# The last layer's two lanes put 33 steps apart instead of 48, with their marks at multiples of three

## The chip, the cores and the metric

The kernel runs on one core of one Trainium2 chip. The time is the device time of one execution in microseconds (us); what counts is the median of several executions.

## What is computed

Four transformer-like layers over 256 tokens of width 2048, batch 1, in float32. Only the fourth (`odd_layer`) is touched by the change. Cut to what matters:

```python
def odd_layer(x, ...):
    proj = rmsnorm(x, norm_g) @ w_in
    xc, zc, qd, kd, vd, zd, a_pre, b_pre = split_cols(proj, OD_SIZES)
    xconv = causal_dwconv(xc, conv_c_w) + conv_c_b
    yc = rg_lru(xconv, gate_w, gate_b, lam) * silu(zc)
    q, k, v = split(silu(causal_dwconv(concat([qd, kd, vd]), conv_d_w)))
    q, k = l2norm(q), l2norm(k)                       # 8 heads of 128
    od = gated_delta_chunkwise(q, k, v, beta, g)
    yd = rmsnorm(od, onorm_g) * silu(zd)
    return concat([yc, yd]) @ w_out
```

`rg_lru` is an elementwise linear recurrence over the tokens. `gated_delta_chunkwise` needs, for each head, the inverse of a unit lower triangular matrix and then a short chain of products with it.

## The kernel before

**Weights.** Nearly all the work of PE is the product of the activations with weights that come from HBM once. SP fetches them unit by unit (half a MB each, two DMAs) into `raw`. ACT rounds each half of a unit to fp32r (L1359, into `whi`), DVE subtracts it from the original (L1993, into `wlo`), and PE does three products for each block of 128 rows and each of the two token blocks: L676, L677, L678. ACT works three halves ahead of PE and may start on a half once PE is done with the half four before it. SP waits, before it fetches unit u, until DVE has split the last half of unit u-4 (`lo_done`).

**The order is written out by hand.** Every engine has its own program, and in it the main work calls `next(side)` at fixed places. The side is a set of generators. In the last layer it is `lanes(...)`, and one call of it is here called a **step**. With `fine=True` every engine makes four steps for each half of a unit, so PE does three of the big products (L676 to L678) in each step, a `project` (one slab of 512 columns) is 32 steps, and the twelve slabs are steps 0 to 383. Where an engine's side has nothing to do at a step it goes on at once; where it has a semaphore to wait for, the engine waits, with all its later work queued behind it, the main work too. PE does nothing out of this order, nor do ACT and DVE.

**The lanes.** `lanes` has three lists of (step at which it may begin, generator). Lane 0 does the gates, then the recurrences of pairs 0 and 2 (`lru`), then the delta rule of pairs 0 and 2 (`delta`); lane 1 does pairs 1 and 3 in the same way; a pair is two heads. The third list multiplies y by the gate z (`gated`). Inside `lru` and `delta`, `to(n)` waits until the generator's own step n; every engine has the same generator with marks of its own, so they stay in the same order. In `lru`, lane 0 stretches its marks by 4/3 and lane 1 by 2.

**A pair of `delta`, by its own steps before:** PE turns q and k (0) and v (4); DVE does nine convolution taps as pairs of L2620 and the three silus (L2672) from 4 to 29; ACT does the first taps (L1875), the tanhs (L1890), and at 23 the squares of q (L1887), which wait for the silu of k. PE sums squares and does k times k at 30 (L1250, L1255), and turns v at 36. At 34 DVE reads the decays (L2696, L2697, L2700), which it needs from DRAM; ACT takes their exponentials at 37 (four L1896, eight of L1904 and L1902). PE does the q-k products at 42 and 49 (L1262 to L1264); the one at 49 waits for DVE's four L2723. From 56 the inverse is built in six rounds. A round l is a product "z" (L1236, with four transposes L1285 behind it from the second round on), a mask by DVE (L2738), a product "t" (L1236), and copies by ACT (L1912 of t, L1916 of the transposes). z stands at 53+6l and t at 56+6l, so each product comes three steps after the one before it, and between them one other engine must have done its part. Then come the solves at 96, 99, 102 (L1295, L1300, L1305) and the output product at 107 (L1312); DVE ends the pair at 114 (L2769), and the lane's next pair waits for that.

**The decays.** `decays` is a small DRAM tensor; each pair needs one row of it on all partitions, in a tile `B` that lies where the pair's convolution inputs were. SP issues that copy (L636) between weight units, at the units numbered 24, 30, 39 and 45 of the layer for pairs 0 to 3:

```python
                if u >= 4:
                    sp.wait_ge(lo_done, 2 * (u - 4) + 2)
                ...
                if u in decays_at:
                    pair = decays_at.index(u)
                    sp.wait_ge(rows_out[1], 16)
                    sp.wait_ge(*dl_d[pair % 2].at(pair // 2, "vc"))
                    sp.dma_start(flat(L3.lane[pair % 2].B), row(decays[2 * pair], 2 * S)).then_inc(dec_in[pair], 16)
```

Half h of the layer's slabs is split by DVE just before its step 4(h-3)+2, and unit n's wait is for half 2n-7. So the copies can go out from steps 8n-38 on: 154, 202, 274 and 322. `vc` is the last tap of v, at the pair's own step 22.

**Gates.** `gated(n)` is one DVE operation over 128x1024 (L2844) at steps 302, 324, 356 and 388, and two over 128x512 (L2852) two steps later (much later for the last). The tanh before it is ACT's L1971.

Of the kernel before, what the change touches and what calls it, by code (L numbers as in the profile page):

```python
# [102 lines left out]
def lanes(gates, delta, lru, gated):  # L103

    lane = [[(0, gates()), (40, lru(0)), (86, lru(2)), (132, delta(0)), (250, delta(2))],
            [(48, lru(1)), (114, lru(3)), (180, delta(1)), (298, delta(3))],
            [(302, gated(0)), (324, gated(1)), (356, gated(2)), (388, gated(3))]]
    tick = 0  # L110
    while any(lane):
        for side in lane:
            if side and tick >= side[0][0] and next(side[0][1], "over") == "over":
                del side[0]
        tick += 1
        yield
# [44 lines left out]
def build_program(nc, a, out, layers=(0, 1, 2, 3)):  # L161
    assert tuple(layers) == (0, 1, 2, 3)
    ctx = ExitStack()
    with ctx:
# [499 lines left out]
        def tensor(pe):  # L664
# [563 lines left out]
            def delta(pair):  # L1228
# [12 lines left out]
                for n in range(3):  # L1241
                    if n == 2:
                        yield from to(4)
                        pe.wait_ge(*v3_a.at(r, "v"))
                        pe.wait_ge(*da.at(r, "cp0"))
                    four(b + n % 2, lambda hh, tb: v.staged[:, n, tb, hh * P:(hh + 1) * P]).then_inc(*dp.up(f"turn{n}"))
# [21 lines left out]
                behind_keys(0, b).then_inc(*dp.up("qk0"))  # L1268
                yield from to(49)
                pe.wait_ge(*dd.at(r, "ad"))  # L1270
                behind_keys(1, b + 1).then_inc(*dp.up("qk1"))
                yield from to(56)
                pe.wait_ge(*dd.at(r, "m"))
# [5 lines left out]
                for l in range(1, 7):  # L1279
                    yield from to(53 + 6 * l)  # L1280
                    pe.wait_ge(*da.at(r, f"mt{l - 1}"))
                    four_by_four(b, v.AD, v.Mt).then_inc(*dp.up(f"z{l}"))
                    if l > 1:
                        for n in range(4):
                            m = pe.transpose(ps[:, b + 1, n * P:(n + 1) * P], v.Mt[:, n, :], ident[:, :])  # L1285
                        m.then_inc(*dp.up(f"d{l - 1}"))
                    yield from to(56 + 6 * l)
                    pe.wait_ge(*dd.at(r, f"z{l}"))
                    if l > 1:
                        pe.wait_ge(*da.at(r, f"m{l - 1}"))  # L1290
                    four_by_four(b, v.M, v.Z).then_inc(*dp.up(f"t{l}"))
# [14 lines left out]
                m.then_inc(*dp.up("u1"))  # L1306
                yield from to(107)
                pe.wait_ge(*dd.at(r, "u1"))
# [36 lines left out]
        def scalar(act):  # L1345
# [511 lines left out]
            def delta(pair):  # L1857
# [47 lines left out]
                m.then_inc(*da.up("ext"))  # L1905
                yield from to(56)
                act.wait_ge(*dp.at(r, "mt"))
                act.copy(flat(v.Mt), ps[:, b, :]).then_inc(*da.up("mt0"))
                for l in range(1, 7):
                    yield from to(56 + 6 * l)  # L1910
                    act.wait_ge(*dp.at(r, f"t{l}"))
                    act.copy(flat(v.Mt), ps[:, b, :]).then_inc(*da.up(f"mt{l}"))  # L1912
                    if l < 6:
                        yield from to(58 + 6 * l)
                        act.wait_ge(*dp.at(r, f"d{l}"))
                        act.copy(flat(v.M), ps[:, b + 1, :]).then_inc(*da.up(f"m{l}"))  # L1916
# [66 lines left out]
        def vector(dve):  # L1983
# [670 lines left out]
            def delta(pair):  # L2654
# [80 lines left out]
                for l in range(1, 7):  # L2735
                    yield from to(53 + 6 * l)
                    dve.wait_ge(*dp.at(r, f"z{l}"))
# [14 lines left out]
                dve.tensor_copy(v.u[:, :, 1], two(b)).then_inc(*dd.up("u1"))  # L2752
                yield from to(107)
                dve.wait_ge(*dp.at(r, "o"))
# [297 lines left out]
```

## Time and profile before

| | |
|---|---|
| median of 3 runs | 2406.24 us (2406.13 to 2406.74) |
| the profiled execution | 2405.99 us |
| its span in the trace | 2404.3 us |
| TensorE's granted clock | 1.0 of full speed |
| PE busy | 2394.9 us (100%) |
| DVE busy | 1478.7 us (62%) |
| ACT busy | 1185.3 us (49%) |
| POOL busy | 150.6 us (6%) |
| mean DMA rate | 174 GB/s |

The span leaves out 1.7 us of start and end that lie around it. Busy times are sums over an engine's instructions; since one instruction's record can reach into the next one's, the distance from start to start is what an instruction takes of its engine when they stand back to back.

### The profile page before, as it was taken

What the parts mean: (1) busy time and instruction counts of PE and PEld (TensorE: products, weight loads), DVE (VectorE), ACT (ScalarE), POOL (GpSimd) and SP (SyncE); (2) the same over time, 40 slices, a digit from 0 to 9 for tenths busy, and PEclk for the clock granted to TensorE, in tenths of its full rate; (3) what the DMA queues carried; (4) which work ended last, traced back from release to release, by engine and by line L of the source; (5) the groups of instructions that cost most, each with busy time, mean ns of one, the idle gap of its engine ahead of it and who ended that gap; (6) DMA issues with size and microseconds to landing.
All of it is one profiled execution on the core that took longest, in us unless ns stands there. A gap on an engine that the chain in (4) does not pass through costs nothing.

```text
span 2404.3 us, 31344 instructions
## 1 busy us (share of the span) xinstructions
PE 2394.9 (100%) x12582; PEld 2043.7 (85%) x12582; DVE 1478.7 (62%) x1982; ACT 1185.3 (49%) x1641; POOL 150.6 (6%) x130
## 2 busy tenths in 40 slices
PE   9999999999999999999999999999999999999999
PEld 8888888888888888878899878888888888888887
DVE  6757575757575757575556576555445566757754
ACT  5454444444444444445455456455444368745543
POOL 0201010101010101000000000000000010000000
PEclk9999999999999999999999999999999999999999
DMA  8555555555555555556654556555555565534444
GB/s 265 177 174 189 197 184 169 186 169 186 168 186 169 185 168 175 194 165 198 189 144 136 193 158 202 179 178 194 176 177 173 173 198 164 160 124 128 127 140 140
DMA packets 369278, 418.26 MB, mean 174 GB/s; under 512 B 28198, under 2 KB 298764, under 8 KB 368620
## 3 DMA queue, kind: packets, MB, share of 16 engines
q1 hardware_dynamic: 367788, 409.36, 52.5%
q0 software_dynamic: 1344, 6.89, 0.8%
q8 instruction: 99, 1.62, 0.3%
q14 instruction: 47, 0.39, 0.1%
HBM read 414.09 MB, written 2.11 MB: 173 GB/s over the span
## 4 chain that ended last, share of the span: by engine, by line
PE 97%; DVE 1%; ACT 1%; issue 0%; POOL 0%; DVEq 0%; POOLq 0%; ACTq 0%
PE ps L676 19%; PE ps L678 19%; PE ps L677 19%; PE ps L707 15%; PE ps L706 7%; PE ps L1236 2%; PE ps L748 2%; PE ps L960 1%; PE ps L949 1%; PE ps L1012 1%; PE ps L1013 1%; PE ps L1011 1%; PE ps L954 1%; PE ps L779 1%; PE ps L781 0%; PE ps L780 0%
## 5 line engine op out<-in xcount | busy, mean ns | idle before, releaser
L1993 DVE TENSOR_TENSOR wlo<-raw,whi 128x1024 fp32r<-128x1024 f32 (+1 forms) x760 | 943.6, 1251 | 611.2 <-ACT whi L1359 608.1
L1359 ACT CAST whi<-raw 128x1024 fp32r<-128x1024 f32 (+1 forms) x766 | 793.3, 1041 | 703.2 <-PE ps L678 522.9
L676 PE MATMUL ps<-whi,xx 128*128 128x512 f32 x2064 | 821.8, 398 | 0.0
L678 PE MATMUL ps<-whi,xx 128*128 128x512 f32 x2064 | 805.2, 390 | 0.0
L677 PE MATMUL ps<-wlo,xx 128*128 128x512 f32 x2064 | 803.8, 389 | 0.0
L707 PE MATMUL ps<-xx,whi 128*128 128x512 f32 x1536 | 538.6, 396 | 0.2 <-DVE wlo L1993 0.2
L678 PEld LDWEIGHTS ps<-whi,xx 128*128 128x128 f32 x2064 | 387.4, 188 | 82.7
L677 PEld LDWEIGHTS ps<-wlo,xx 128*128 128x128 f32 x2064 | 388.2, 188 | 75.6
L676 PEld LDWEIGHTS ps<-whi,xx 128*128 128x128 f32 x2064 | 387.9, 188 | 74.8
L706 PE MATMUL ps<-xx,wlo 128*128 128x256 f32 x1440 | 405.4, 282 | 0.0
L707 PEld LDWEIGHTS ps<-xx,whi 128*128 128x128 f32 x1536 | 286.2, 188 | 63.3 <-issue 0.4
L706 PEld LDWEIGHTS ps<-xx,wlo 128*128 128x128 f32 x1440 | 271.6, 189 | 2.0
L2900 POOL TENSOR_TENSOR work<-work 128x512 f32<-128x512 f32 x48 | 96.7, 2014 | 830.1 <-DVE work L2335 627.2
L1501 ACT ACTIVATE work<-work,small 128x128 f32<-128x128 f32 (+1 forms) x80 | 44.4, 555 | 143.3 <-DVE small L2233 143.3
L2331 DVE TENSOR_TENSOR work<-work 64x512 f32<-64x512 f32 x96 | 88.4, 921 | 2.2
L1605 ACT COPY work<-ps 128x512 f32<-128x512 f32 x48 | 28.0, 584 | 59.9 <-PE ps L707 59.9
L2370 DVE TENSOR_TENSOR work<-work,ps 128x512 f32<-128x512 f32 x48 | 33.0, 687 | 36.7 <-ACT work L1605 36.7
L1236 PEld LDWEIGHTS ps<-work 128*128 128x128 f32 x384 | 49.7, 191 | 5.0 <-ACT work L1912 1.3
L1236 PE MATMUL ps<-work 128*128 128x128 f32 x384 | 50.9, 275 | 0.3
L2230 DVE CUSTOM_DVE_ANT_0 work<-ps,work 128x128 f32<-128x128 f32 (+1 forms) x80 | 36.0, 488 | 21.0 <-PE ps L949 15.6
L1011 PE MATMUL ps<-xx,whi 128*128 128x256 f32 x160 | 48.1, 301 | 0.0
L1013 PE MATMUL ps<-xx,whi 128*128 128x256 f32 x160 | 45.2, 283 | 0.0
(428 smaller groups left out, 1897.8 us busy)
## 6 DMA issues: line engine op xcount, KB each, us to landing
raw<-in_dsa_w_in SPq DMA_DIRECT2D x320, 512.0 KB, 4.4
raw<-in_ev_w_in SPq DMA_DIRECT2D x144, 512.0 KB, 4.4
raw<-in_od_w_in SPq DMA_DIRECT2D x96, 512.0 KB, 4.6
raw<-in_mla_w_in SPq DMA_DIRECT2D x48, 512.0 KB, 4.5
raw<-in_dsa_w_out SPq DMA_DIRECT2D x32, 512.0 KB, 4.7
raw<-in_mla_w_out SPq DMA_DIRECT2D x32, 512.0 KB, 4.8
raw<-in_ev_w_out SPq DMA_DIRECT2D x32, 512.0 KB, 4.5
raw<-in_od_w_out SPq DMA_DIRECT2D x32, 512.0 KB, 4.8
```

The source lines that it names most:

```text
L676: pe.matmul(o, xh[:, k, tokens[tb]], hi, start=start and s + l == 0, stop=False)
L677: pe.matmul(o, xh[:, k, tokens[tb]], lo, start=False, stop=False)
L678: m = pe.matmul(o, xl[:, k, tokens[tb]], hi, start=False, stop=stop and s + l == 2)
L706: pe.matmul(ps[:, bank + c, 0:S], lo[:, t, cols], xh[:, k, :], start=False, stop=False)
L707: m = pe.matmul(ps[:, bank + c, :], hi[:, t, cols], xx[:, :, k, :], start=k == 0, stop=k == KT - 1)
L1011: pe.matmul(o, hi, xh[:, k, :], start=first and g != 1, stop=False)
L1013: m = pe.matmul(o, hi, xl[:, k, :], start=False, stop=last and g != 0)
L1236: m = pe.matmul(ps[:, bank, n * P:(n + 1) * P], left[:, n, :], right[:, n, :], start=True, stop=True)
L1359: act.copy(half_of_weights(h)[0][:, :, 0:n] if n > FEW else few_high(h, n), whole_half(raw[:, u % 4, 2 * (h % 2):2 * (h % 2) + 2], n)).the ...
L1993: dve.tensor_tensor(lo[:, :, 0:n] if n > FEW else few_low(h, n), whole_half(raw[:, h // 2 % 4, 2 * (h % 2):2 * (h % 2) + 2], n), hi.bitcas ...
L2331: m = dve.tensor_tensor(L0.t2[a_], L0.h[b_, n], bc(L0.sina[b_], 1, 2), ALU.mult)
L2900: pool.tensor_tensor(L0.t1, L0.h[:, n], bc(L0.cosa, 1, 2), ALU.mult).then_inc(*p0_g.up(f"cos{n}"))
```

## The change

Two things are edited, both of them only numbers that say at which step something stands. In `lanes`, `lru(2)`, `delta(0)` and `delta(2)` of lane 0 start at 89, 138 and 255 instead of 86, 132 and 250, and `lru(1)`, `lru(3)`, `delta(1)` and `delta(3)` of lane 1 at 40, 105, 171 and 288 instead of 48, 114, 180 and 298. So the delta pairs are 33 steps apart, which was 48. Inside `delta` the marks of PE's products go to multiples of three, with the marks of DVE and ACT that belong to them: v is turned at 3, the second q-k product stands at 48, the first transposes at 57, z at 54+6l, t at 57+6l, the output product at 108. No instruction is added, taken away or changed in size, and `decays_at` and the steps of `gated` stay.

```diff
-    lane = [[(0, gates()), (40, lru(0)), (86, lru(2)), (132, delta(0)), (250, delta(2))],
-            [(48, lru(1)), (114, lru(3)), (180, delta(1)), (298, delta(3))],
+    lane = [[(0, gates()), (40, lru(0)), (89, lru(2)), (138, delta(0)), (255, delta(2))],
+            [(40, lru(1)), (105, lru(3)), (171, delta(1)), (288, delta(3))],
             [(302, gated(0)), (324, gated(1)), (356, gated(2)), (388, gated(3))]]
...
                     if n == 2:
-                        yield from to(4)
+                        yield from to(3)
                         pe.wait_ge(*v3_a.at(r, "v"))
...
-                yield from to(49)
+                yield from to(48)
                 pe.wait_ge(*dd.at(r, "ad"))
                 behind_keys(1, b + 1).then_inc(*dp.up("qk1"))
-                yield from to(56)
+                yield from to(57)
                 pe.wait_ge(*dd.at(r, "m"))
...
                 for l in range(1, 7):
-                    yield from to(53 + 6 * l)
+                    yield from to(54 + 6 * l)
                     pe.wait_ge(*da.at(r, f"mt{l - 1}"))
...
-                    yield from to(56 + 6 * l)
+                    yield from to(57 + 6 * l)
                     pe.wait_ge(*dd.at(r, f"z{l}"))
...
-                yield from to(107)
+                yield from to(108)
                 pe.wait_ge(*dd.at(r, "u1"))
```

ACT's marks of the same loop go from 56+6l and 58+6l to 57+6l and 59+6l, DVE's from 53+6l to 54+6l and from 107 to 108.

**Where the instructions go.** On SP nothing moves. On PE the number of places at which the layer's big products are interrupted by small ones falls from 108 to 85, since products of both lanes now stand at the same place 23 times. Three places show what moves on DVE and ACT.

DVE around `gated(0)` (step 302), where pair 2 is past its four L2723. Before (L2730 and L2734 are pair 2's, L2620 pair 3's taps):

```order
L2730 TENSOR_TENSOR work<-ps,work 128x512 [waits dl_a0,dl_p0]
L1993 TENSOR_TENSOR wlo<-raw,whi 128x1024 [waits hi_done]
L2734 TENSOR_TENSOR work<-work 128x512 [waits dl_g0]
L2730 TENSOR_TENSOR work<-ps,work 128x512 [waits dl_a0,dl_p0]
L1993 TENSOR_TENSOR wlo<-raw,whi 128x1024 [waits hi_done]
L2620 SCALAR_TENSOR_TENSOR work<-work,vec 128x256 [waits dl_a1]
L2620 SCALAR_TENSOR_TENSOR work<-work,vec 128x256
L2844 SCALAR_TENSOR_TENSOR work<-work,ps 128x1024 [waits z3_a]
L2620 SCALAR_TENSOR_TENSOR work<-work,vec 128x256 [waits z3_d,dl_d1,rg_a1,rg_a0]
L2620 SCALAR_TENSOR_TENSOR work<-work,vec 128x256
L2852 SCALAR_TENSOR_TENSOR y<-work,hrstd,y 128x512 x2
```

Now:

```order
L2620 SCALAR_TENSOR_TENSOR work<-work,vec 128x256 [waits dl_a1]
L2620 SCALAR_TENSOR_TENSOR work<-work,vec 128x256
L2730 TENSOR_TENSOR work<-ps,work 128x512 [waits dl_a0,dl_p0]
L2620 SCALAR_TENSOR_TENSOR work<-work,vec 128x256 [waits dl_d1]
L2620 SCALAR_TENSOR_TENSOR work<-work,vec 128x256
L1993 TENSOR_TENSOR wlo<-raw,whi 128x1024 [waits hi_done]
L2620 SCALAR_TENSOR_TENSOR work<-work,vec 128x256 [waits dl_d1]
L2620 SCALAR_TENSOR_TENSOR work<-work,vec 128x256
L2844 SCALAR_TENSOR_TENSOR work<-work,ps 128x1024 [waits z3_a]
L2672 SCALAR_TENSOR_TENSOR work<-work 128x512 [waits dl_a1,dl_d1]
L2734 TENSOR_TENSOR work<-work 128x512 [waits z3_d,dl_g0,rg_a1,rg_a0]
L2852 SCALAR_TENSOR_TENSOR y<-work,hrstd,y 128x512 x2
```

Before, pair 3 had just begun here and two of its three taps of q are shown; now its taps of k and v and its silu of q stand among the same work of pair 2, and an L1993 fewer lies between.

ACT around the first copy of pair 2's inverse (L1908). Before:

```order
L1875 ACTIVATE work<-work,vec 128x256 [waits dl_a1]
L1875 ACTIVATE work<-work,vec 128x256
L1908 COPY work<-ps 128x512 [waits dl_p0]
L1890 ACTIVATE work<-work 128x512 [waits dl_d1]
L1359 CAST whi<-raw 128x1024 [waits half_done,raw_in3]
L1912 COPY work<-ps 128x512 [waits dl_p0]
L1359 CAST whi<-raw 128x1024 [waits half_done,raw_in3]
L1916 COPY work<-ps 128x512 [waits dl_p0]
L1890 ACTIVATE work<-work 128x512 [waits dl_d1]
```

Now:

```order
L1890 ACTIVATE work<-work 128x512 [waits dl_d1]
L1359 CAST whi<-raw 128x1024 [waits half_done,raw_in2]
L1359 CAST whi<-raw 128x1024 [waits half_done,raw_in3]
L1887 ACTIVATE work<-work 128x512 [waits dl_d1]
L1908 COPY work<-ps 128x512 [waits dl_p0]
L1890 ACTIVATE work<-work 128x512 [waits dl_d1]
L1359 CAST whi<-raw 128x1024 [waits half_done,raw_in3]
L1359 CAST whi<-raw 128x1024 [waits half_done,raw_in0]
L1912 COPY work<-ps 128x512 [waits dl_p0]
```

Before, the first taps of pair 3 (L1875) stood ahead of that copy; now the squares of pair 3's q (L1887) do, which wait for DVE's silu of k (`dl_d1`).

DVE around the split for which SP waits before it fetches pair 3's decays. Before, the six rows from that L1993 on; pair 3's L2696 comes 16 rows further down:

```order
L1993 TENSOR_TENSOR wlo<-raw,whi 128x1024 [waits hi_done]
L2844 SCALAR_TENSOR_TENSOR work<-work,ps 128x1024 [waits z3_a]
L1993 TENSOR_TENSOR wlo<-raw,whi 128x1024 [waits z3_d,hi_done,rg_a1,rg_a0]
L2852 SCALAR_TENSOR_TENSOR y<-work,hrstd,y 128x512 x2
L2738 TENSOR_TENSOR work<-ps,work 128x512 [waits dl_p0]
L2672 SCALAR_TENSOR_TENSOR work<-work 128x512 [waits dl_a1,dl_d1]
```

Now:

```order
L2738 TENSOR_TENSOR work<-ps,work 128x512 [waits dl_p0]
L1993 TENSOR_TENSOR wlo<-raw,whi 128x1024 [waits hi_done]
L2696 TENSOR_TENSOR small<-work 128x2 [waits dl_d1,dec_in3]
L2697 SCALAR_TENSOR_TENSOR work<-work 128x512
L2700 TENSOR_TENSOR work<-work 128x2x128 x2
L2844 SCALAR_TENSOR_TENSOR work<-work,ps 128x1024 [waits z3_a]
L2708 SCALAR_TENSOR_TENSOR small<-small,work 128x4 [waits dl_g1]
L2710 SCALAR_TENSOR_TENSOR small<-small 128x4 [waits dl_d1]
L2712 TENSOR_SCALAR small<-small 128x2 [waits dl_d1]
L2713 TENSOR_SCALAR small<-small 128x4
L1993 TENSOR_TENSOR wlo<-raw,whi 128x1024 [waits z3_d,hi_done,rg_a1,rg_a0]
L2716 TENSOR_TENSOR work<-ps,small 128x512 [waits dl_p1]
```

The second row is the same L1993. L2696, which waits for the decays (`dec_in3`), now stands right behind it, with L2844, the next L1993, L2716 and L2852 behind that and pair 2's next L2738 after them.

## Rows read from the trace of the kernel before

**Rows 1.** The page: its first line, and the chain that ended last.

```profile
span 2404.3 us, 31344 instructions
...
PE 97%; DVE 1%; ACT 1%; issue 0%; POOL 0%; DVEq 0%; POOLq 0%; ACTq 0%
```

**Rows 2.** Groups by line, PE, last layer (busy, mean ns | idle before, releaser).

```profile
L1236 PE MATMUL ps<-work 128*128 128x128 f32 x384 | 50.9, 275 | 0.3
...
L748 PE MATMUL ps<-ident,work 128*128 128x128 f32 x80 | 11.3, 272 | 0.5 <-DVE y L2769 0.5
```

**Rows 3.** PE in order of time: a side product and the big products behind it.

```profile
2097.28 1.05 PE L1236 MATMUL ps<-work 128*128 128x128 f32 x8
2098.08 0.48 PE L676 MATMUL ps<-whi,xx 128*128 128x512 f32 x1
2098.40 0.39 PE L677 MATMUL ps<-wlo,xx 128*128 128x512 f32 x1
2098.63 0.39 PE L678 MATMUL ps<-whi,xx 128*128 128x512 f32 x1
```

**Rows 4.** PE in order of time: output product joined across lanes, and one alone.

```profile
2149.48 1.50 PE L1312 MATMUL ps<-work 128*128 128x128 f32 x12
2150.82 1.06 PE L1236 MATMUL ps<-work 128*128 128x128 f32 x8
...
2202.03 1.50 PE L1312 MATMUL ps<-work 128*128 128x128 f32 x12
2203.28 0.48 PE L676 MATMUL ps<-whi,xx 128*128 128x512 f32 x1
```

**Rows 5.** DVE in order of time: three kinds of work back to back.

```profile
2181.36 0.69 DVE L2672 SCALAR_TENSOR_TENSOR work<-work 128x512 f32<-128x512 f32 x1
2181.97 1.22 DVE L1993 TENSOR_TENSOR wlo<-raw,whi 128x1024 fp32r<-128x1024 f32 x1
2183.10 1.80 DVE L2620 SCALAR_TENSOR_TENSOR work<-work,vec 128x256 f32<-128x256 f32 x4
2184.89 0.69 DVE L2738 TENSOR_TENSOR work<-ps,work 128x512 f32<-128x512 f32 x1
```

**Rows 6.** ACT in order of time: the exponentials of pair 3 (eight follow 2252.48).

```profile
2252.48 1.28 ACT L1896 ACTIVATE work<-work 128x128 f32<-128x128 f32 x4
2253.66 0.39 ACT L1904 ACTIVATE work<-work,small 128x128 f32<-128x128 f32 x1
...
2256.00 0.57 ACT L1912 COPY work<-ps 128x512 f32<-128x512 f32 x1
2256.47 1.05 ACT L1359 CAST whi<-raw 128x1024 fp32r<-128x1024 f32 x1
```

**Rows 7.** SP, PE and DVE around the decays of pair 3.

```profile
2239.36 0.34 SPq L636 DMA_DIRECT2D work<-decays  x1
...
2235.01 1.05 PE L1236 MATMUL ps<-work 128*128 128x128 f32 x8
...
2236.10 0.69 DVE L2738 TENSOR_TENSOR work<-ps,work 128x512 f32<-128x512 f32 x1 [1.23 <-PE ps L1236]
2238.11 1.23 DVE L1993 TENSOR_TENSOR wlo<-raw,whi 128x1024 fp32r<-128x1024 f32 x1 [1.31 <-ACT whi L1359]
2239.25 1.22 DVE L2844 SCALAR_TENSOR_TENSOR work<-work,ps 128x1024 f32<-128x1024 f32 x1
...
2247.68 0.16 DVE L2696 TENSOR_TENSOR small<-work 128x2 f32<-128x2 f32 x1
...
2248.37 0.75 DVE L2700 TENSOR_TENSOR work<-work 128x256 f32<-128x256 f32 x2
```

**Rows 8.** DMA issues of the last layer (KB each, median us to landing).

```profile
work<-decays SPq DMA_DIRECT2D x4, 256.0 KB, 4.3
```

**Rows 9.** Groups by line, DVE, last layer.

```profile
L2723 DVE SCALAR_TENSOR_TENSOR work<-ps,small,work 128x128 f32<-128x128 f32 x16 | 4.5, 343 | 0.0
...
L2852 DVE SCALAR_TENSOR_TENSOR y<-work,hrstd,y 128x512 f32<-128x512 f32 x8 | 5.6, 747 | 0.0
```

More of the change, by code:

```diff
@@ L1905, in delta @@
                 m.then_inc(*da.up("ext"))
-                yield from to(56)
+                yield from to(57)
                 act.wait_ge(*dp.at(r, "mt"))
@@ L1909, in delta @@
                 for l in range(1, 7):
-                    yield from to(56 + 6 * l)
+                    yield from to(57 + 6 * l)
                     act.wait_ge(*dp.at(r, f"t{l}"))
@@ L1913, in delta @@
                     if l < 6:
-                        yield from to(58 + 6 * l)
+                        yield from to(59 + 6 * l)
                         act.wait_ge(*dp.at(r, f"d{l}"))
@@ L2735, in delta @@
                 for l in range(1, 7):
-                    yield from to(53 + 6 * l)
+                    yield from to(54 + 6 * l)
                     dve.wait_ge(*dp.at(r, f"z{l}"))
@@ L2752, in delta @@
                 dve.tensor_copy(v.u[:, :, 1], two(b)).then_inc(*dd.up("u1"))
-                yield from to(107)
+                yield from to(108)
                 dve.wait_ge(*dp.at(r, "o"))
```

## The prediction

> **What bounds the kernel now.** I read the page first: PE is the chain that ended last in 97% of a span of 2404.3 us [rows 1], so the time is PE's own work plus what PE waits. Then the groups by line, for PE's waits in the last layer: 0.5 at L748, where pair 3's first turn waits for pair 1's L2769, 0.3 at L1236 [rows 2], and some 0.2 more spread over single rows. About 1.0 us is all that better marks could take from the waits. Then PE in order of time, for what an interruption costs: the 8 products of a z or t take 0.80, and the L676 behind them starts its successor 0.32 later where L677 has 0.23, so a return to the big products costs 0.09; a step of three big products is 3 x 0.228 = 0.685 [rows 3]. Last DVE, ACT and SP around pair 3, since the change moves lane 1's start onto busy stretches of lane 0.
>
> **Joining the lanes' products** (108 places become 85). If each of the 23 places saved that 0.09, it would be 2.1 us. The trace has such a joint already: the output product with the other lane's L1236 behind it takes 1.34, the same product with L676 behind it 1.25 [rows 4]. The 0.09 is thus paid at the border between the lanes too, and joining saves nothing but the restart of the big product, some hundredths at a few places. I take 0.1 in all; bounds 0 and 2.1. The Trainium skill (TensorE: Matmul & The Clock Gate, "Part 2: What happens when you issue a matmul") says that products in a stream cost only their columns and an isolated one shows its drain; by it the joins would be worth the 2.1, and the sum below would be 14.6 in place of 16.6.
>
> **The waits of before.** Pair 2's four L2723 (1.1) stood on DVE in the steps just ahead of pair 1's L2769; with lane 1 fifteen steps earlier against lane 0 they now come after it, a silu (0.61) is there, and the 0.5 at L748 goes. The other 0.5 I count as gone too: -1.0.
>
> **New stalls.** What replaces them comes from one fact. Lane 1's first own steps are its dearest for DVE and ACT (nine tap pairs, three silus, twelve first taps, three tanhs). 48 steps behind, they lay where lane 0 was in its inverse, which leaves DVE free. 33 behind, own steps 0 to 24 of lane 1 are 33 to 57 of lane 0: its decays, exponentials, L2723s and copies. What one thing costs, start to start: a silu or other 128x512 op 0.61, a split L1993 1.13, a tap pair 0.80 (1.79 for two, with a wait, at the row shown) [rows 5]; L2844 1.14, as L1993; four L2723 1.1, an L2852 0.67 of the 0.75 shown [rows 9]; on ACT the exponentials 3.5 (1.18 for four, 2.34 for eight), a copy 0.47, a cast 0.95 (1.05 busy) [rows 6].
>
> *A. Pairs 2 and 3, steps 288 to 318* (time 0 where PE begins step 288).
> (1) The second q-k product, at step 303. PE gets there after 15 steps (10.3), 20 small products at 0.11 (2.2) and the restarts: 12.9. DVE: split done 3.8; small ones 0.5, a tap pair, L2716: 5.75. The next split waits for a cast that stands on ACT behind two copies and a cast (2.6), four first taps (1.7), the exponentials (3.5) and a copy: cast done 9.3, split 10.45. Then two tap pairs 1.6, another split 1.15, four L2723 1.1: 14.3. Stall 1.4 at L1262.
> (2) z1 at step 315. DVE goes on with five tap pairs (4.0), five 128x512 ops (3.0: L2730, L2734, silus of q and k among them), L2844 1.14, two L2852 1.33, two splits 2.3: 26.1. Only then can ACT take L1887, the squares, which wait for the silu of k and now stand ahead of L1908, the copy that z1 needs: 27.2. PE is due at 12.9 + 1.4 + 0.9 + nine steps 6.2 + 0.4 + three steps 2.05 = 23.9. Stall 3.3 at L1236.
> (3) z1's mask stands behind the tanh of v, a cast and a split: 31.5, against t1 due at 30.15. Stall 1.4.
> A comes to 6.1. Its bounds: each of the three is the difference of sums of some twenty terms; with the taps at the 0.90 of the row shown it is 7.5, with DVE never waiting for a cast 3.
>
> *B. The decays of pair 3.* SP issues them right after a split (L636 at 2239.36, a little after the L1993 of 2238.11 to 2239.34, itself 4.35 after PE's L1236 at 2235.01), they land 4.3 later [rows 7, 8], at about 2243.7, and L2696 runs at 2247.68: slack 4.0. The units' numbers have not moved, so the issue stays tied to the split before step 322. Pair 3's own step 34 does move, from 332 to 322. L2696 is now the next thing on DVE after the very split for which SP waits, so all of the 4.3 is a wait of DVE, with pair 2's masks queued behind it. From the start of t1 at step 318: t1 0.9, pair 3's two groups of that size 1.8, three steps 2.05, so z2 starts at 4.75; issue +4.35 = 9.1; landing 13.4; L2696 to the end of L2700 1.44 [rows 7], L2844 1.14, small ones 0.5, split 1.14, L2716 0.6, two L2852 1.33, z3's mask 0.7: 20.3. PE wants t3, at step 330, at 14.9 (t1, the 1.8, z2 and z3 with their transposes 1.34 each, t2 0.9, pair 3's turn 0.44, twelve steps 8.2). Stall **5.4**; with a landing between 3.9 and 4.4, 5.0 to 5.5. If DVE had nothing else between L2700 and the mask, still 0.6. The Trainium skill (DMA: Bandwidth & Descriptors, "Anatomy of one DMA — SWDGE (gpsimd) path") gives 2.0 us and bytes over 436e3; as an estimate, 2.6 for these 256 KB. Row 8's 4.3 was measured for this transfer on another queue, so it decides; by the rule B would be 3.7 and the sum 14.9.
>
> *C. Pairs 0 and 1, steps 171 to 213.* The same mechanism without L2844, L2852: z1 (step 198) waits for lane 1's silu of k 1.55, t1 0.4; t3 (step 213) waits 1.35, because the exponentials of pair 1 (3.5) stand ahead of a cast, that ahead of a split, that ahead of z3's mask. 3.3. Pair 1's decays are issued at step 202 for use at 205, with less behind them: nothing. Bounds 0 and 5.
>
> *D. Small ones.* Step 126 0.2; step 161 0.8 (lru(3)'s scan behind delta(0)'s taps on DVE); step 261 0.6 (pair 1's fifth inverse copy behind first taps and a cast); step 273 0.1; steps 360 and 363 1.2 (ACT's copy of the transposes is queued ahead of L1421, for which DVE's work ahead of the mask waits). 2.9, bounds 1 and 5.
>
> SP waits for `vc` some six steps longer in pairs 0 and 2; the unit that is held up is needed twenty steps later, since four are in flight. If a stall there did reach the casts, that would be a microsecond.
>
> **Sum.** 6.1 + 5.4 + 3.3 + 2.9 = 17.7, less 1.0 and 0.1: +16.6. On the profiled execution's 2405.99 that is 2422.6; it lies 0.25 below the median, which the range swallows. Below 4.8 us (0.2%) a measurement of this kernel can hardly tell a difference from none.
>
> **Rivals.**
> *R1, not slower:* the joins are worth 0.09 each and DVE keeps up. It decides at the silu of k: if DVE has done it before PE's step 315 (23.9 on the scale of A, I have 26.1), L1887 doesn't hold L1908, and if the slack of the decays is eaten by an earlier split, B goes too. For it: DVE is at 62% over the span, and 2.2 us is within the error of A. Against it: rows 4, and B, which needs no sum to be seen. 2406.0 - 2.1 - 1.0 = 2402.9, or 2405 without the joins' worth. Chance 0.08.
> *R2:* only the decays' wait is real, since DVE catches up within lane 0's idle steps: 5.4 - 1.1, 2410.3; with a C of 1 it is 2411. Chance 0.14.
> *R3, stalls compound:* what is late on ACT delays casts, casts delay splits, and the next delta stage meets them. Each of A, C and D at its upper bound: 7.5 + 5.5 + 5 + 5 - 1.1 = +21.9, 2428; and if each stall is followed by one like A(3) in the next round (1.4 each, four rounds), 2433. Chance 0.14. Against it: a stall of PE gives the others time, so it usually mends.
> *Forecast:* 0.64.
>
> **Numbers.** Predicted 2422.6. The forecast's own range is 2415 to 2428; taking in R2 and most of R3, 2409 to 2432. Faster by over 0.2% needs the better half of R1: 0.03. Within 0.2% (up to 2411.0) are the rest of R1 and most of R2, with a little: 0.14. Slower 0.83.
>
> **What the profile after would show.** PE's busy time unchanged within 1 us (if it falls by 2, the joins pay and I was wrong on them). On PE, idle time at L1236 of 10 us or more where it had 0.3: waits for ACT's L1908 near steps 198 and 315, for DVE's L2738 near 213, 318 and 330; 1.4 at L1262 for L2723; none at L748 for L2769. On DVE, a wait of some 4 us at L2696 for the decays of pair 3. If L2696 doesn't wait, B is wrong; if L1908 is done before PE asks, A(2) and C are. What would make the prediction wrong as a whole is a DVE that passes own steps 0 to 24 of lane 1 without being late.

## The result, and the profile after

The changed kernel takes 2424.78 us (median of 5 runs, 2424.40 to 2425.92) against 2406.56 for the kernel before in the same comparison: 18.2 us more, ratio 1.0076 with a 95% interval of 1.0065 to 1.0088. The forecast was 2422.6, in a range of 2409 to 2432.

The page of the changed kernel, first line, busy times and chain, beside [rows 1]:

```profile
span 2424.2 us, 31344 instructions
...
PE 2400.0 (99%) x12582; PEld 2047.2 (84%) x12582; DVE 1478.8 (61%) x1982; ACT 1184.5 (49%) x1641; POOL 150.8 (6%) x130
...
PE 93%; DVE 3%; ACT 2%; issue 1%; DMA 1%; SPq 0%; POOL 0%; DVEq 0%; ACTq 0%
```

DVE and ACT do what they did before, within 1 us. PE's chain has waits in it now (an idle stretch in which PE waits for another engine is called a stall), and its busy time has grown by 5.1 us (2394.9 before) for the same number of instructions. The forecast did not have that second part.

The waits of PE in the last layer, from the view of waits (in all, times, longest):

```profile
PE ps L1236 <- DVE work L2738: 6.8, 2, 5.7
PE ps L1236 <- ACT work L1908: 5.1, 2, 3.4
PE ps L1262 <- DVE work L2723: 1.3, 1, 1.3
PE ps L1223 <- DVE work L2650: 1.1, 2, 0.8
PE ps L1236 <- ACT work L1912: 0.4, 1, 0.4
```

They come to 14.7 us (14.6 by the rows in order of time) where the kernel before had 0.3 at L1236, 0.5 at L748 [rows 2] and 0.2 at L1262. The 0.5 at L748 is gone. In order of time on PE, with the idle time before each in brackets:

```profile
2105.66 1.16 PE L1236 MATMUL ps<-work 128*128 128x128 f32 x8 [1.69 <-ACT work L1908]
...
2125.31 1.16 PE L1236 MATMUL ps<-work 128*128 128x128 f32 x8 [1.07 <-DVE work L2738]
...
2183.52 1.16 PE L1236 MATMUL ps<-work 128*128 128x128 f32 x8 [0.36 <-ACT work L1912]
...
2223.54 0.49 PE L1262 MATMUL ps<-work 128*128 128x128 f32 x2 [1.31 <-DVE work L2723]
...
2236.74 1.36 PE L1236 MATMUL ps<-work 128*128 128x128 f32 x8 [3.41 <-ACT work L1908]
2237.76 0.77 PE L676 MATMUL ps<-whi,xx 128*128 128x512 f32 x1
2238.33 0.63 PE L677 MATMUL ps<-wlo,xx 128*128 128x512 f32 x1
2238.76 0.63 PE L678 MATMUL ps<-whi,xx 128*128 128x512 f32 x1
...
2262.28 2.08 PE L1236 MATMUL ps<-work 128*128 128x128 f32 x8 [5.72 <-DVE work L2738]
```

These are steps 198, 213, 261, 303, 315 and 330, in this order; two more of 0.2 and 0.8 stand at L1223, steps 126 and 161. Behind the 3.41 the big products come 0.43 apart and take 0.63, against 0.23 and 0.39 [rows 3]: TensorE runs at its lower clock. The view by stretches shows it as the column behind the five engines (PEclk, 1.00 in every stretch of the kernel before up to PE's last product):

```profile
2220.00:2230.00 10.00, 8.69 (x41) 6.96 (x40) 9.96 (x20) 3.67 (x6) 0.74 (x1) 1.00 0.32 107
2230.00:2240.00 10.00, 6.59 (x30) 5.25 (x29) 8.37 (x14) 4.12 (x6) 0.00 (x0) 0.88 0.34 106
2240.00:2250.00 10.00, 10.00 (x63) 8.88 (x62) 5.24 (x16) 3.41 (x6) 1.65 (x1) 0.95 0.36 107
2250.00:2260.00 10.00, 6.56 (x40) 5.43 (x38) 4.99 (x12) 4.64 (x13) 0.00 (x0) 1.00 0.49 131
2260.00:2270.00 10.00, 7.72 (x32) 6.90 (x33) 4.39 (x9) 2.51 (x5) 0.64 (x1) 0.66 0.36 105
```

The missing share by the length is 0.12 x 10 + 0.05 x 10 at the stall of 3.41, and 0.34 x 10 at the one of 5.72, 5.1 us in all. All other stretches up to PE's last product show 1.00. I call such a piece a **dip** from here on and give its size in this way. It costs that much only where PE has work: in stretches of 0.25 us the clock is at 0.50 from 2237.5 to 2241.0 and from 2261.4 to 2268.3, and PE comes back from the second stall at 2262.28, so 0.4 of the 3.4 falls into the stall itself and costs nothing. The loss is 4.7 us. PE's busy time without any dip lies within 1.1 us of 2394.9 in the runs below, so its extra 5.1 agrees with either figure.

So the profiled execution adds up: waits 14.7 less the 1.0 of before, 4.7 lost by the dips, and 1.2 more at the start of the program for the first load of the input (2.1 against 0.9, which is no matter of the change): 19.6, where the spans differ by 19.9. That execution is 1.1 us above the median.

SP and DVE at the decays of pair 3, in order of time, beside [rows 7]:

```profile
2249.26 1.23 DVE L1993 TENSOR_TENSOR wlo<-raw,whi 128x1024 fp32r<-128x1024 f32 x1 [1.31 <-ACT whi L1359]
...
2250.52 0.34 SPq L636 DMA_DIRECT2D work<-decays  x1
...
2255.43 0.16 DVE L2696 TENSOR_TENSOR small<-work 128x2 f32<-128x2 f32 x1 [4.94 <-DMA work<-decays]
...
2256.11 0.75 DVE L2700 TENSOR_TENSOR work<-work 128x256 f32<-128x256 f32 x2
2256.78 1.21 DVE L2844 SCALAR_TENSOR_TENSOR work<-work,ps 128x1024 f32<-128x1024 f32 x1
...
2258.47 1.22 DVE L1993 TENSOR_TENSOR wlo<-raw,whi 128x1024 fp32r<-128x1024 f32 x1
2259.62 0.68 DVE L2716 TENSOR_TENSOR work<-ps,small 128x512 f32<-128x512 f32 x1
2260.22 1.41 DVE L2852 SCALAR_TENSOR_TENSOR y<-work,hrstd,y 128x512 f32<-128x512 f32 x2
2261.54 0.68 DVE L2738 TENSOR_TENSOR work<-ps,work 128x512 f32<-128x512 f32 x1
```

The copy is issued as the split before step 322 ends, DVE has nothing ahead of L2696 and waits 4.94, and the list of work behind it, up to the mask for which PE stands, is the one of the forecast's part B.

DVE and ACT ahead of step 315, the forecast's part A:

```profile
2214.35 0.69 DVE L2716 TENSOR_TENSOR work<-ps,small 128x512 f32<-128x512 f32 x1
2218.39 1.22 DVE L1993 TENSOR_TENSOR wlo<-raw,whi 128x1024 fp32r<-128x1024 f32 x1 [3.35 <-ACT whi L1359]
...
2234.88 0.68 DVE L2672 SCALAR_TENSOR_TENSOR work<-work 128x512 f32<-128x512 f32 x1
2235.48 1.21 DVE L1993 TENSOR_TENSOR wlo<-raw,whi 128x1024 fp32r<-128x1024 f32 x1
...
2235.59 0.63 ACT L1887 ACTIVATE work<-work 128x512 f32<-128x512 f32 x1 [5.06 <-DVE work L2672]
2236.12 0.57 ACT L1908 COPY work<-ps 128x512 f32<-128x512 f32 x1
```

DVE stands idle for 3.35 while ACT does the exponentials, is then busy without a gap up to the silu of k at 2234.88, and ACT, idle for 5.06 in its turn, does the squares and only then the copy that PE wants. The 3.41 is all here.

### The profile page after: what moved, and what is told of

The parts are those of the page before. It is cut to its first block, busy times and chain, and to the rows that moved or that the text cites. A ratio compares the mean times of both kernels' runs of the same rounds, so it can differ in the third digit from the quotient of the medians.

```text
span 2424.2 us, 31344 instructions
## 1 busy us (share of the span) xinstructions
PE 2400.0 (99%) x12582; PEld 2047.2 (84%) x12582; DVE 1478.8 (61%) x1982; ACT 1184.5 (49%) x1641; POOL 150.8 (6%) x130
## 4 chain that ended last, share of the span: by engine, by line
PE 93%; DVE 3%; ACT 2%; issue 1%; DMA 1%; SPq 0%; POOL 0%; DVEq 0%; ACTq 0%
PE ps L676 18%; PE ps L678 18%; PE ps L677 18%; PE ps L707 15%; PE ps L706 7%; PE ps L1236 2%; PE ps L748 1%; PE ps L960 1%; PE ps L949 1%; PE ps L1012 1%; PE ps L1011 1%; PE ps L1013 1%; DVE wlo L1993 1%; ACT whi L1359 1%; DVE work L2620 1%
## 5 line engine op out<-in xcount | busy, mean ns | idle before, releaser
L1993 DVE TENSOR_TENSOR wlo<-raw,whi 128x1024 fp32r<-128x1024 f32 (+1 forms) x760 | 942.9, 1250 | 612.5 <-ACT whi L1359 609.2
L676 PE MATMUL ps<-whi,xx 128*128 128x512 f32 x2064 | 820.9, 398 | 0.0
L676 PEld LDWEIGHTS ps<-whi,xx 128*128 128x128 f32 x2064 | 388.7, 188 | 76.0
L1236 PEld LDWEIGHTS ps<-work 128*128 128x128 f32 x384 | 49.6, 194 | 17.4 <-DVE work L2738 8.2
L1236 PE MATMUL ps<-work 128*128 128x128 f32 x384 | 52.0, 280 | 12.3 <-DVE work L2738 6.8
```

Of the source, the lines that this page charges most:

```text
L676: pe.matmul(o, xh[:, k, tokens[tb]], hi, start=start and s + l == 0, stop=False)
L1236: m = pe.matmul(ps[:, bank, n * P:(n + 1) * P], left[:, n, :], right[:, n, :], start=True, stop=True)
L1993: dve.tensor_tensor(lo[:, :, 0:n] if n > FEW else few_low(h, n), whole_half(raw[:, h // 2 % 4, 2 * (h % 2):2 * (h % 2) + 2], n), hi.bitcas ...
```

## The experiments

Two theories stood against each other at the start. Mine: the 33 steps between the lanes put DVE's and ACT's dearest work of lane 1 onto lane 0's, the late decays add to it, and joining the products saves nothing. The rival: the new marks themselves matter, by joins that save time or by putting both lanes' demands on one step. A third question came with the result: whether the dips follow from the stalls. All times are medians, beside the kernel before on the same chip (2406.45 in the first four, 2406.95 in the next four, 2406.63 in the last three). "Waits" are sums over PE's rows of the last layer.

**1. Pair 3's decays one unit earlier**

```diff
-        decays_at = [widths.index(16) + 1 + n for n in (24, 30, 39, 45)]
+        decays_at = [widths.index(16) + 1 + n for n in (24, 30, 39, 44)]
```

> The changed kernel, with pair 3's decays issued one unit earlier (44 in place of 45), so behind the split before step 314 and eight steps ahead of L2696. My theory (the 5.7 at PE's L1236 is the landing of the decays, 4.9 at DVE's L2696 for it, and the slow clock behind it, 2.9, is the price of that stall): both go, L2696 waits for no DMA, 2424.8 - 8.6 = 2416.2. Rival 1 (the slow clock has another cause than the stall): only 5.7 goes, 2419.1, and the granted clock still falls near step 330. Rival 2 (DVE is saturated there and the decays were only the last thing to come): L2738's stall shrinks to 2 or so, 2421.

2418.57 us (2417.57 to 2419.01). Every stall before step 318 is the same to 0.01 us, the 5.72 has become 0.69, and the dip behind it is gone; the one behind the 3.41 stays (1.7 lost).

```profile
2236.30 1.16 PE L1236 MATMUL ps<-work 128*128 128x128 f32 x8 [3.41 <-ACT work L1908]
...
2256.76 1.16 PE L1236 MATMUL ps<-work 128*128 128x128 f32 x8 [0.69 <-DVE work L2738]
```

Of the 18.2 us, 6.2 hung on this one number. Expected were 8.6. The two profiled executions differ by 8.4 (5.0 less of waiting, 3.4 less of dip). The medians differ by less, and this kernel's executions fall into two groups: 2417.57 (the profiled one) and 2418.18 with a mean granted clock of 0.999 over the span, 2418.96 and 2419.01 with 0.998, so presumably with more of dips, which only a profile of theirs could show. Rivals 1 and 2 are out: the dip went with its stall, and L2738's wait went to 0.69 and not to 2.

**2. The marks alone**

```diff
-    lane = [[(0, gates()), (40, lru(0)), (86, lru(2)), (132, delta(0)), (250, delta(2))],
-            [(48, lru(1)), (114, lru(3)), (180, delta(1)), (298, delta(3))],
+    lane = [[(0, gates()), (40, lru(0)), (86, lru(2)), (132, delta(0)), (249, delta(2))],
+            [(48, lru(1)), (114, lru(3)), (180, delta(1)), (297, delta(3))],
```

in the kernel before, with the changed kernel's marks inside `delta`; 96 places in place of 108.

> The kernel before with the new marks (multiples of three) and the lanes still 48 steps apart, delta(2) at 249 and delta(3) at 297: 96 places at which small products interrupt the big ones instead of 108, without the new congestion. My theory (joining saves nothing): 2406.5, within 0.4 but for the wait at L748, which may grow from 0.5 to 1.5 since the lane's next pair has one step less. Rival (each join saves 0.09): PE busy 1.1 less and 2405.4.

2406.74 us against 2406.45, ratio 1.0001 (0.9992 to 1.0010). PE's waits are 0.6 at L748 and 0.3 at L1236, as before, and PE's busy time is 2395.7, not 1.1 below 2394.9. Twelve joins bring nothing that shows here, but the interval is some 2 us wide to either side and busy times of kernels alike in this vary by 1, so the run alone could not exclude 1.1. The trace of the changed kernel settles it, where a z or t of one lane stands right behind one of the other:

```profile
2146.73 1.95 PE L1236 MATMUL ps<-work 128*128 128x128 f32 x16
2148.44 0.48 PE L676 MATMUL ps<-whi,xx 128*128 128x512 f32 x1
2148.75 0.40 PE L677 MATMUL ps<-wlo,xx 128*128 128x512 f32 x1
```

The two groups and the L676 behind them take 2.02. One group and its L676 take 1.12 [rows 3]; two of those, less the 0.23 of one big product that stands once here and not twice, make 2.01. A saved restart of 0.09 would leave 1.92. The join saves nothing.

**3. The offset alone**: the kernel before with the changed kernel's two lines of starts, and none of its marks inside `delta`.

```diff
-    lane = [[(0, gates()), (40, lru(0)), (86, lru(2)), (132, delta(0)), (250, delta(2))],
-            [(48, lru(1)), (114, lru(3)), (180, delta(1)), (298, delta(3))],
+    lane = [[(0, gates()), (40, lru(0)), (89, lru(2)), (138, delta(0)), (255, delta(2))],
+            [(40, lru(1)), (105, lru(3)), (171, delta(1)), (288, delta(3))],
```

> The kernel before with its own marks and the lanes 33 steps apart (all starts as in the changed kernel). My theory (the offset alone makes the stalls): L1236 waits for L1908 near step 197 and 314 and for L2738 near 329, L2696 waits some 4 to 5 for the decays, the clock falls twice, and the time is 2422 to 2427. Rival (the marks, which put both lanes' products at one step, make the stalls): within 3 us of 2406.5.

2425.88 us (2422.57 to 2426.14), 1.1 above the changed kernel. The stalls are of the same kind, some at other places:

```profile
2220.13 0.49 PE L1262 MATMUL ps<-work 128*128 128x128 f32 x2 [0.62 <-DVE work L2723]
...
2226.95 0.66 PE L1276 MATMUL ps<-ident,work 128*128 128x128 f32 x4 [0.89 <-DVE work L2734]
...
2237.57 2.07 PE L1236 MATMUL ps<-work 128*128 128x128 f32 x8 [4.92 <-DVE work L2738]
...
2262.02 2.07 PE L1236 MATMUL ps<-work 128*128 128x128 f32 x8 [4.72 <-DVE work L2738]
```

PE waits 13.0 in all, and its busy time is 2402.4. The offset makes the loss, the marks don't. Of what I expected, the waits for L1908 did not come: with the old marks ACT takes L1908 one step earlier, ahead of the squares, and PE is stopped by the masks instead (run 5 does the same to the changed kernel).

**4. The same wait of DVE where little is queued behind it**

```diff
-        decays_at = [widths.index(16) + 1 + n for n in (24, 30, 39, 45)]
+        decays_at = [widths.index(16) + 1 + n for n in (24, 30, 39, 46)]
```

in the kernel before.

> The kernel before with pair 3's decays issued one unit later (46 in place of 45), behind the split before step 330, with L2696 at step 332. L2696 then waits some 4.3 on DVE as in the changed kernel, but between the masks of two rounds and with little queued behind. My theory (a wait of DVE costs what PE lacks at the next product, not its own length): a stall of 0.5 to 2 at L1236, no slow clock, 2407 to 2409. Rival (the landing costs its own length wherever it stands): 2411, and with a slow clock 2414.

2408.18 us, 1.7 more than before, with stalls of 1.10 and 0.29 at L1236 and no dip.

```profile
2253.35 0.16 DVE L2696 TENSOR_TENSOR small<-work 128x2 f32<-128x2 f32 x1 [4.78 <-DMA work<-decays]
...
2254.70 0.68 DVE L2738 TENSOR_TENSOR work<-ps,work 128x512 f32<-128x512 f32 x1
```

L2696 waits 4.78, and the mask starts 1.4 after it, where in the changed kernel 6.1 lie between them. The same transfer, waited for in the same queue, costs 1.7 here and over 6 in the changed kernel (by run 1, 5.0 of waiting and the rest by the dip): what counts is the list behind it and how much room PE had.

**5. The squares behind the other lane's copy**, in the changed kernel.

```diff
                     if kind == "v":
-                        yield from to(23)
+                        yield from to(25)
                         act.wait_ge(*dd.at(r, "sk"))
```

> The changed kernel with ACT's squares of q (L1887) at a pair's own step 25 in place of 23, so that the other lane's first copy L1908 stands ahead of them. PE then no longer waits for L1908 (1.69 and 3.41 gone). If the squares' place in the queue were the cause (theory Q), the two stalls go with it: 2424.8 - 5.1 - 1.7 (slow clock) = 2418. If DVE's load is the cause (theory D, mine), the wait passes to the next round's mask: z1's L2738 stands behind the same taps, silu and splits, about 3 at t1 of pair 2 where it was 3.4 at z1, 0 to 1 for pair 0: 2422 to 2424.

2428.89 us (2424.30 to 2429.41), worse. The waits did what theory D says: those for L1908 are gone, and the next round's mask takes their place with 1.86 (1.69 before) and 2.95 (3.41 before); together PE waits 13.8 in place of 14.7. For pair 0 the wait is longer than the 0 to 1 expected. The time was not as expected either: the dips have grown from 5.1 to 8.5, and what they cost from 4.7 to 8.4.

```profile
2100.00:2110.00 10.00, 8.14 (x43) 6.71 (x42) 9.49 (x16) 5.82 (x8) 0.00 (x0) 0.96 0.55 169
2110.00:2120.00 10.00, 10.00 (x50) 9.10 (x49) 3.64 (x16) 2.01 (x3) 1.64 (x1) 0.70 0.55 174
```

The stall of 1.86 ends at 2108.96, and where the changed kernel's 1.69 brought no dip, this one, hardly longer, has 3.4. So the squares' place was not the cause, and my number failed because I priced the stalls alone.

**6. The exponentials in two pieces**, in the changed kernel.

```diff
                 m.then_inc(*da.up("ex"))
+                yield from to(39)
                 for hh in range(2):
```

> The changed kernel with ACT's eight L1904/L1902 of a pair at its own step 39 in place of right behind the four L1896 at 37, so that a cast L1359 goes ahead of them. Theory D (DVE falls behind because it sits idle 3.35 for the cast behind 3.5 of exponentials, then is saturated): that idle time falls to about 1, the 1.31 at L1262 goes, z1's stall near step 315 shrinks from 3.4 to 2.4, the 1.07 at step 213 goes, the slow clock behind 315 shortens: 2420 to 2421.5. Rival (the exponentials cost DVE nothing that it needs): all stalls as in the changed kernel, 2424.8.

2420.52 us, with PE's waits at 10.2. The 1.31 at L1262 is 0.21, the 1.07 at step 213 is gone, and the 1.69 at step 198 too, which I had not expected. The 3.41 is still 3.38. The order of time on DVE says why:

```profile
2213.11 1.22 DVE L1993 TENSOR_TENSOR wlo<-raw,whi 128x1024 fp32r<-128x1024 f32 x1 [1.02 <-ACT whi L1359]
2214.25 1.79 DVE L2620 SCALAR_TENSOR_TENSOR work<-work,vec 128x256 f32<-128x256 f32 x4
2217.19 1.23 DVE L1993 TENSOR_TENSOR wlo<-raw,whi 128x1024 fp32r<-128x1024 f32 x1 [1.15 <-ACT whi L1359]
```

The idle 3.35 has become 1.02 and then 1.15, for the next cast, which now stands behind the eight exponentials. DVE comes 1.1 earlier out of it; PE, rid of a stall of 1.1, comes 1.1 earlier too, and the distance between them stays. So the time fell into my range for partly other reasons than mine: of what I expected, neither the stall near step 315 nor the low clock at it got shorter (the low clock lasted 6.8 where it had lasted 3.4), and the 1.69 went instead.

**7. Three edits at once** (1, 5 and 6).

> The changed kernel with all three edits: decays of pair 3 at unit 44, squares at own step 25, the eight exponentials at 39. Theory D: what is left is 0.2 and 0.8 at L1223, 0.4 at step 261, and one stall of about 2 near step 318 with little slow clock: 2409 to 2412. Never below the kernel before, since the joins bring nothing. Rival (joins worth 0.09 each, hidden until now by stalls): 2407 to 2410 with PE busy 2 us below the kernel before.

2414.82 us. Waits: 0.20, 0.85, 0.35, 0.21, one of 2.96 for L2738 near step 318, and 0.69; with the dip of 3.4 behind the 2.96 that is 5.3 - 0.7 + 3.4 = 8.0, measured 7.9. It missed my range because the one stall left is 1.0 longer than the 2 expected and has a full dip where I had little. The rival is out too: PE's busy time, 2398.7, is not below the kernel before, with or without the dip.

**8. Lanes 42 steps apart**, against the changed kernel.

```diff
-            [(40, lru(1)), (105, lru(3)), (171, delta(1)), (288, delta(3))],
+            [(48, lru(1)), (114, lru(3)), (180, delta(1)), (297, delta(3))],
```

> The changed kernel's marks and lane 0, with lane 1 at 48, 114, 180 and 297, so 42 steps behind in place of 33. Theory D: lane 1's first 24 own steps meet lane 0's 42 to 66, past its exponentials; no cast starves, DVE is less late, the decays of pair 3 (own step 34 at 331, issue at 322) have time to land: stalls of 0 to 2 in all and no slow clock, 2406.5 to 2409. Rival (any offset short of 48 puts the taps on the first rounds of the inverse and costs alike, but for the decays): 2414 to 2418.

2411.36 us. `delta` behaves as theory D has it: 0.22 and 0.54 at L1236, no dip. The rest I had not seen: 2.6 at L1223 in three places (0.55, 0.74, 1.32), where the recurrences' transposes wait for DVE's scan, and 1.16 at L748, where pair 3 begins and waits for pair 1's L2769. I take the first to come from `lru` standing in yet another place against the other lane; no run tested either of them. The time lies above the range of theory D and below the rival's.

**9, 10. One isolated stall in the kernel before**

```diff
+                for n in range(10 if pair == 3 else 0):
+                    dve.scalar_tensor_tensor(out=v.AD, in0=v.B, scalar=-1.0, in1=bc(L3.mincl, 1, 4), op0=ALU.mult, op1=ALU.add).then_inc(dec_in[3], 1)
+                    dve.wait_ge(dec_in[3], 17 + n)
                 dve.scalar_tensor_tensor(out=v.AD, in0=v.B, scalar=-1.0, in1=bc(L3.mincl, 1, 4), op0=ALU.mult, op1=ALU.add)
```

and the same with 7.

> The kernel before with DVE's L2697 of pair 3 done ten times more, one after the other (some 0.75 each, 7.5 in all), just ahead of pair 2's next mask: one isolated stall of PE in a kernel that has none. By the order of time the mask ends 3.9 after PE wants it. Theory S (a stall of this length itself brings the slow clock of TensorE): the granted clock falls behind the stall and costs 1.7 to 3.4 more, 2412 to 2414. Rival (the slow clock of the changed kernel comes from its crowded schedule): no fall, 2410.4.

> The same with seven repetitions (5.3): a stall of 1.7, as long as one in the changed kernel behind which the clock stayed (1.69), and as one of the run with the squares moved behind which it fell (1.86). Theory S: near the length at which the clock sometimes falls, 2408 in the executions where it stays and 2410 to 2411.5 where it falls. Rival: 2408 in all.

With ten: 2411.84 us. Three lines more of code put L2738 at L2741. The stall is 3.50, and the clock falls at it, with nothing of the changed kernel around:

```profile
2257.23 2.08 PE L1236 MATMUL ps<-work 128*128 128x128 f32 x8 [3.50 <-DVE work L2741]
```

```profile
2240.00:2250.00 10.00, 10.00 (x65) 8.97 (x64) 8.64 (x21) 3.35 (x5) 2.54 (x1) 1.00 0.57 143
2250.00:2260.00 10.00, 6.50 (x35) 5.52 (x35) 9.10 (x18) 4.92 (x14) 0.00 (x0) 0.80 0.27 93
2260.00:2270.00 10.00, 10.00 (x52) 8.61 (x51) 5.13 (x8) 4.71 (x7) 0.64 (x1) 0.86 0.35 107
...
2255.00:2256.00 1.00, 0.00 (x0) 0.00 (x0) 0.97 (x3) 0.00 (x0) 0.00 (x0) 1.00 0.00 0
2256.00:2257.00 1.00, 0.00 (x0) 0.00 (x0) 1.00 (x3) 0.39 (x2) 0.00 (x0) 0.50 0.00 0
```

A dip of 3.4 in this execution, and it begins 1.2 us before PE comes back at 2257.23, so 2.8 of it is lost; PE's busy time is 2.7 above that of the kernel before. The ten executions lie between 2410.10 (mean granted clock 1.000 of the whole run) and 2412.71 (0.998). Only one was profiled; the clocks of the others (0.998 or 0.999 in all but the fastest) say that the same stall has a dip in most and none in one, and 2410.1 is what the stall alone would give (2406.6 and 3.5). Theory S holds for a stall of this length, with a median just under its range, and the rival is out.

With seven: 2408.52, all ten between 2407.68 and 2408.72 at a clock of 1.000. The stalls are 1.32 and 0.29 and not the 1.7 meant, so this run says nothing of the lengths between 1.69 and 1.86, and it doesn't tell theory S from its rival.

**11. Less work for DVE.** The kernel of run 7, and for pair 3 the first two of the three DVE taps of k and of v on 8 tokens only; that part of the convolution is left out.

```diff
-                        m = tap(j, dst[:, hh], v.cpd[:, 2 * n + hh], vcol("cd", 1, 24 * j + 8 * n + 2 * pair + hh))
+                        short = pair == 3 and n > 0 and j < 3
+                        m = dve.scalar_tensor_tensor(out=dst[:, hh, 0:8], in0=v.cpd[:, 2 * n + hh, L3.PAD - 3 + j:L3.PAD - 3 + j + 8], scalar=vcol("cd", 1, 24 * j + 8 * n + 2 * pair + hh), in1=dst[:, hh, 0:8], op0=ALU.mult, op1=ALU.add) if short else tap(j, dst[:, hh], v.cpd[:, 2 * n + hh], vcol("cd", 1, 24 * j + 8 * n + 2 * pair + hh))
```

> The kernel with all three edits (decays at 44, squares at 25, exponentials at 39), and for pair 3 the first two of the three taps of k and of v done on 8 tokens instead of 256, so four tap pairs, 2.4 us less of DVE ahead of the silu of k: that part of the convolution is left out. Theory D (what PE waits for near step 318 is DVE's load): the stall of 2.96 at L1236 falls to 0.6, the slow clock there goes, 2409. Rival (a cast or copy that waits in line sets it, not DVE's load): the stall stays above 2, 2413 to 2415.

2408.65 us (2408.13 to 2409.45). From the view of waits (L2739 is the mask; one more line of code):

```profile
PE ps L1236 <- DVE work L2739: 1.2, 2, 0.7
```

The stall of 2.96 is 0.49 after 2.4 us of DVE's work were taken away, and the clock is 1.00 up to PE's last product. It is DVE's load. And here, at 85 places and without a dip, PE's busy time is 2395.6, not two below 2394.9; waits 2.8 (with 1.0 at L1223, 0.4 for L1912 and 0.2 for L2724) less the 0.7 of before give 2.1, and the measured difference is 2.0. Nothing is left for the joins to have saved.

## Why the prediction was right, and where it was not

The direction, the mechanism and the places were right; the total came near because one term was missing and three others did not come.

- **Bound.** PE sets the time, and the waits of before were worth 1.0 at most. The last layer's waits of before at L748 and near L1262 are gone as forecast.
- **Joining** (0.1 forecast, 2.1 by the other reading). Right: 0 in the rows of run 2 and in the balance of run 11. The Trainium skill's rule (TensorE: Matmul & The Clock Gate, "Part 2: What happens when you issue a matmul"), that products in a stream cost only their columns, does not help at a border between small products of two lanes: 16 of them take 1.71, twice the 0.80 of eight and 0.1 for the border. [rows 4] had shown it.
- **A(1), the q-k product at step 303**: 1.4 forecast, 1.31 measured.
- **A(2), z1 at step 315**: 3.3 forecast, 3.41 measured, with the squares ahead of the copy and the silu of k at the end of DVE's busy stretch. But run 5 shows that the squares' place is only where the lateness surfaces.
- **A(3), t1 at step 318**: 1.4 forecast, none seen. PE came later to it because of the dip. Its mask ended at 2240.9 and PE came at 2241.4; PE had lost 1.7 in between, so at full clock about 1.2 of stall would have stood there: an estimate from these rows. That it did not come is luck.
- **B, the decays**: 5.4 forecast, 5.72 measured. The landing took 4.9 from issue where I used the 4.3 of [rows 8]. The Trainium skill's formula (DMA: Bandwidth & Descriptors, "Anatomy of one DMA — SWDGE (gpsimd) path") gives 2.6 as an estimate. It is stated for DMAs issued on the gpsimd path; this one goes out on SP's queue and takes 3.8 to 4.9 in the changed kernel, so the measurement decides.
- **C, pairs 0 and 1**: 1.55, 0.4 and 1.35 forecast, 1.69, none and 1.07 measured. Run 6 shows both of them to hang on the exponentials.
- **D**: 0.2, 0.8, 0.6, 0.1 and 1.2 forecast; 0.21, 0.84, 0.36, none and none measured. Why no stall came at steps 360 and 363, no run shows; I suppose that I gave ACT too little room there.
- **The sum of the stalls** was forecast at 17.7 and is 14.7.
- **What the sum lacked: the slow clock.** The step that failed is "PE's busy time unchanged within 1 us". It grew by 5.1. I took a stall at its own length and priced the clock at nothing, without a reason. The two longest stalls brought dips that cost 4.7 us in the profiled execution, a quarter of the whole. The net of the waits was forecast at 16.6 and is 13.7; had the clock stayed, the kernel would have taken about 2421.5, an estimate from 13.7 and the 1.2 of A(3). An error of 3 us one way and one of 5 the other thus stood against each other, and that the total of 2422.6 is so near to the measured 2424.8 is in part luck.
- **Rivals.** R1 needed the silu of k to be done before PE comes to z1; it ended some 2 us after PE's last big product had, and the joins are worth nothing (run 2). R2 (the decays alone) is out by run 1, where 12 us are left without them. R3 (compounding) did not happen in the form given: in run 6 three stalls ahead went (1.69, 1.07 and most of the 1.31), and the 3.41 stayed at 3.38.

What stays open: whether 33 steps could be made free at all by moving DVE's work, and not only by leaving some out. No run tried it. Since the joins save nothing, only the 1.0 of waits in the kernel before was there to win, and no version here beats that kernel. What decides between a dip and none, at stalls as near to each other as 1.69 and 1.86 or in executions of one kernel, is open too.

## What to carry to other kernels

When two interleaved lanes are shifted against each other, write down for each engine what falls on the same steps, and follow every load whose issue is tied to the main stream's count: it does not move with the lane that uses it, and here one such number was worth a third of the loss. The price of a late operand is the wait for it and what stands behind it in the queue, less the room its reader has: the same transfer, waited for in the same queue, cost 1.7 us or 6.2. Where TensorE is the bound, a stall is to be priced with a second term for the clock (in the last layer of these profiles each stall from 1.86 us up had a dip, none of 1.69 or less had), and an edit that only moves a stall can lose by that term: in run 5 fewer microseconds of waiting took more time.

## What the runs showed of the hardware

The granted clock of TensorE fell from 2.4 to 1.2 GHz (0.50 in the stretches) at these stalls of PE, and nowhere else before PE's last product, in brackets the dip: 1.86 (3.4), 2.95 and 2.96 (3.4 each), 3.38 (3.4), 3.41 (1.7, in two kernels), 3.50 (3.4), 4.72 (3.4), 4.92 (5.2), 5.18 (3.4), 5.25 (1.7), 5.72 (3.4). At the many stalls of 0.2 to 1.69 it stayed at 1.00, and also at one of 1.95 at the start of the changed kernel's program, where PE waits for the first input. It fell at moments between 3.1 us before PE came back (the 5.18, run 6) and 1.5 us after (the 3.41, run 1). The part of a dip that lies in the stall costs nothing: the 3.4 at the 5.18 cost 1.9, the 3.4 at the 3.50 cost 2.8, the 5.2 at the 4.92 cost 4.8. What a dip costs does not follow the length of the stall, and it seems to differ between executions of the same kernel: in run 9 the ten executions span 2.6 us, and the fastest has a granted clock of 1.000. Kernels with dips spread more: 2422.57 to 2426.14 in run 3 and 2424.30 to 2429.41 in run 5, against 2407.68 to 2408.72 in run 10, which has no dip.
